# A hybrid decoder layer on one core: transposes two steps behind the scores, query tiles in the order 1, 3, 0, 4, 7, 6, 5, 2, w_out copied from step 6 and output pieces from step 15

## The reference, cut to what matters

```python
h = rmsnorm(x, norm_g) * (1.0 + scale) + shift        # shift, scale, gate from silu(c) @ ada_w + ada_b
z = h @ w_in                                          # x: 1024 rows (tokens) x 1024
xr, gr, q, k, v, ga, qi, ki, wi = split(z)
y_r = rg_lru(causal_conv(xr)) * silu(gr)              # 512 channels
# for each block of 128 queries, 8 heads of 64:
score = sum_h relu(qi_h . ki) * wi_h                  # indexer; causal
idx = top_k(score, 256)                               # keys that a query may see
p = softmax(q . k[idx] * 64 ** -0.5)                  # only those keys
y_a = (p @ v[idx]) * silu(ga)
y = concat([y_r, y_a]) @ w_out                        # 1024 x 1024
out = rmsnorm(x + gate * y, final_g)
```

## Time and profile before

| what | value |
|---|---|
| median of three runs | 598.59 us |
| the profiled execution | 599.06 us |
| its span, first to last instruction | 597.3 us |
| PE busy | 539.3 us, 90% |
| DVE, ACT, POOL busy | 419.9, 388.9, 211.3 us |
| first score of the attention stage | 340.59 us |
| first output piece | 400.67 us |
| last matmul ends | 590.0 us |

### The profile page before, as it was taken

The page is one execution under the profiler, slowest core; times in us unless marked ns, Lnnn a source line. Parts: engine busy times, 40 slices in busy tenths (PEclk is TensorE's granted clock), DMA queues, the critical chain, the costliest instruction groups (busy, mean ns, idle before and its releaser), DMA issues.

```text
span 597.3 us, 8271 instructions
## 1 busy us (share of the span) xinstructions
PE 539.3 (90%) x2756; PEld 447.6 (75%) x2758; DVE 419.9 (70%) x993; ACT 388.9 (65%) x690; POOL 211.3 (35%) x190
## 2 busy tenths in 40 slices
PE   0499988999999999989999866699999999999995
PEld 0477667888687777778888655678898989888874
DVE  4765659888989889998898757464566656664532
ACT  4572724554498898988898675673657566656631
POOL 6522044031436253588464000580412030314222
PEclk9869999999999999999999959679999999999998
DMA  8993094241011112134452160200102010101011
GB/s 304 397 326 102 19 253 165 57 106 36 12 61 36 36 36 52 48 99 120 106 130 82 29 254 1 82 26 1 41 31 72 1 59 13 42 31 71 1 72 70
DMA packets 19658, 51.98 MB, mean 87 GB/s; under 512 B 4128, under 2 KB 5152, under 8 KB 19616
## 3 DMA queue, kind: packets, MB, share of 16 engines
q1 hardware_dynamic: 19616, 51.45, 27.2%
HBM read 37.81 MB, written 4.19 MB: 70 GB/s over the span
## 4 chain that ended last, share of the span: by engine, by line
PE 73%; DVE 10%; ACT 6%; issue 5%; POOL 2%; DMA 2%; SPq 1%; DVEq 0%; POOLq 0%; ACTq 0%
PE pair L1542 28%; PE pair L1683 14%; PE pair L1705 6%; PE pair L1718 5%; PE pair L1511 4%; PE pair L1647 3%; PE pair L1648 2%; PE pair L1619 2%; DVE score_sb L1365 2%; PE pair L1727 2%; PE pair L1610 2%; PE pair L1611 1%; PE pair L1488 1%; PE pair L1743 1%; DVE tie L1299 1%
## 5 line engine op out<-in xcount | busy, mean ns | idle before, releaser
L1450 DVE TENSOR_TENSOR pt_lo<-pair,pt_hi 128x512 fp32r<-128x512 f32 (+3 forms) x96 | 50.5, 554 | 71.5 <-ACT pt_hi L1060 70.9
L955 ACT ACTIVATE bias_sb<-score_sb,tinies 128x1024 bf16<-128x1024 f32 (+2 forms) x93 | 95.7, 1032 | 4.2 <-DVE tinies L1234 3.9
L1542 PE MATMUL pair<-h_hi,w_hi 128*128 128x512 f32 x304 | 97.8, 403 | 0.0
L1542 PE MATMUL pair<-h_lo,w_hi 128*128 128x512 f32 x304 | 93.9, 390 | 0.0
L1542 PE MATMUL pair<-h_hi,w_lo 128*128 128x512 f32 x304 | 93.6, 389 | 0.0
L1220 DVE TENSOR_SCALAR_CACHE_REDUCE bias_sb<-score_sb,tinies 128x640 bf16<-128x640 f32 (+2 forms) x93 | 72.4, 801 | 0.8
L756 POOL TENSOR_SCALAR w_hi<-w_raw 128x1024 fp32r<-128x1024 f32 (+1 forms) x22 | 23.3, 1060 | 136.2 <-DMA w_raw<-in_w_tiles 115.3
L1542 PEld LDWEIGHTS pair<-h_hi,w_hi 128*128 128x128 f32 x304 | 56.3, 188 | 14.7 <-issue 4.6
L1542 PEld LDWEIGHTS pair<-h_lo,w_hi 128*128 128x128 f32 x304 | 57.1, 188 | 12.3
L1542 PEld LDWEIGHTS pair<-h_hi,w_lo 128*128 128x128 f32 x304 | 57.1, 188 | 12.2
L1060 ACT ACTIVATE pt_hi<-pair 128x512 fp32r<-128x512 f32 (+3 forms) x96 | 43.5, 489 | 28.2 <-PE pair L1718 25.9
(11 more groups left out here) (213 smaller groups left out, 1311.8 us busy)
## 6 DMA issues: line engine op xcount, KB each, us to landing
w_raw<-in_w_tiles SPq DMA_DIRECT2D x21, 512.0 KB, 4.0
ada<-in_ada_w SPq DMA_DIRECT2D x16, 512.0 KB, 12.1
x_sb<-in_x SPq DMA_DIRECT2D x8, 512.0 KB, 8.6
ada_g<-in_ada_w SPq DMA_DIRECT2D x8, 512.0 KB, 5.5
qs<-half_hi SPq DMA_DIRECT2D x16, 256.0 KB, 3.8
qs<-half_lo SPq DMA_DIRECT2D x16, 256.0 KB, 4.7
wo_raw<-in_w_out SPq DMA_DIRECT2D x8, 512.0 KB, 7.3
x_res<-in_x SPq DMA_DIRECT2D x8, 512.0 KB, 3.4
```

What stands on the lines that cost most here:

```text
L955: nc.scalar.activation(junk[i], score_sb[:, SCORE_OFF[i]:SCORE_OFF[i] + keys_of(i)], ACT.Sign, bias=cand[:, c:c + 1], scale=-1.0, accum_ou ...
L1450: nc.vector.tensor_tensor(pt_lo[:, 4 * b:4 * b + nc4, hh, :], psum[use % 2][:, 0:nc4 * P].rearrange("p (c q) -> p c q", q=P), f32(pt_hi[:, ...
L1542: ins = nc.tensor.matmul(psum[banks[half]][0:width, :], w[b][:, k, 0:width], hh[:, k, half * HALF:(half + 1) * HALF], start=(k == 0 and p ...
```

## The change

The lag of the transposes, and all lags that hang on it, grow by one step, so LAST_STEP goes from 77 to 78. The order of tiles becomes 1, 3, 0, 4, 7, 6, 5, 2: tile 3 (512 keys) takes steps 8 to 15, tile 0 (128 keys) 16 to 23, tile 4 (640 keys) 24 to 31. wo_hi copies run in steps 6 to 13. Output pieces begin at step 15 with pieces 0 and 1, and go on with one a step, piece g - 14, to step 77; yr_hi of the first two tiles moves to step 11. DVE waits at the first step of a tile for that tile's own mask alone, PE still for all six at the first step of tile 4, now step 24. prob_early grows to 512 keys, and the second tie_t buffer moves for it. fg_bc and yg lie over the queries of the tiles 1 and 3. ACT's Square writes its values, which nobody reads, into yg as float32 instead of a bfloat16 buffer, and DVE therefore waits before it writes yg again for that Square rather than for POOL's add.

```diff
@@ -98,11 +98,11 @@
-ATT = [1, 0, 4, 7, 6, 5, 3, 2]
-LAG_T = 1
+ATT = [1, 3, 0, 4, 7, 6, 5, 2]
+LAG_T = 2
 LAG_PV = LAG_T + 2
 LAG_O = LAG_T + 3
 LAG_Y = LAG_T + 10
@@ -115,8 +115,8 @@
 FLIP_AT = {3 + n: c for n, c in enumerate(MASK_ORDER)}
 RANK_AT = {4 + n: c for n, c in enumerate(MASK_ORDER)}
 BIAS_AT = {5 + n: c for n, c in enumerate(MASK_ORDER)}
-WO_START = 10
-OUT_START = 20
+WO_START = 6
+OUT_START = 15
 PIECES = {g: [2 * (g - OUT_START), 2 * (g - OUT_START) + 1] for g in range(OUT_START, 2 * OUT_START - LAG_OUT)}
 PIECES.update({g: [g - LAG_OUT] for g in range(2 * OUT_START - LAG_OUT, LAST_STEP)})
 PIECES.update({LAST_STEP - 8 + n: [56 + o] for n, o in enumerate((0, 1, 4, 5, 2, 3, 6, 7))})
@@ -375,7 +375,7 @@
         w_lo = [sb(f"w_lo{b}", R_W + 4096 * b, [P, KC, P], F32R) for b in range(3)]
         w_hi = [sb(f"w_hi{b}", R_W + 12288 + 4096 * b, [P, KC, P], F32R) for b in range(3)]
         prob = [sb(f"prob{b}", R_W + 4096 * b, [P, S]) for b in range(2)]
-        prob_early = sb("prob_early", R_W + 2048, [P, keys_of(1)])
+        prob_early = sb("prob_early", R_W + 2048, [P, keys_of(3)])
         pt_hi = sb("pt_hi", R_W + 8192, [P, NT, 2, P], F32R)
         pt_lo = sb("pt_lo", R_W + 16384, [P, NT, 2, P], F32R)
@@ -417,14 +417,12 @@
         gate_b = sb("gate_b", R_R + 4096, [P, D])
         v_raw = sb("v_raw", R_R + 8192, [P, NT, HD])
         tri = sb("tri", R_R, [P, S], BF16)
-        tie_t = [sb("tie_t0", R_R + 2048, [P, S], BF16), sb("tie_t1", R_W + 5120, [P, S], BF16)]
+        tie_t = [sb("tie_t0", R_R + 2048, [P, S], BF16), sb("tie_t1", R_W + 6144, [P, S], BF16)]
         x_res = [sb("x_res0", R_R, [P, D]), sb("x_res1", R_S, [P, D])]
         yr_hi = [sb(f"yr_hi{b}", R_S + 4096 + 2048 * b, [P, CT, P], F32R) for b in range(2)]
         pv_sb = [sb(f"pv{b}", R_R + 4096 + 1024 * b, [P, 2, P]) for b in range(2)]
         o_sb = sb("o_sb", R_R + 6144, [P, NH * HD])
         prob_late = sb("prob_late", R_S + 12288, [P, S])
-        sq_junk = sb("sq_junk", R_S + 16384, [P, HALF], BF16)[:, :]
         at = (R_R + 8192, R_S + 8192)
         ya_hi = [sb(f"ya_hi{b}", at[b], [P, 4, P], F32R) for b in range(2)]
         ya_raw = [sb(f"ya_raw{b}", at[b] + 2048, [P, 4, P]) for b in range(2)]
@@ -448,8 +446,8 @@
         gate_bc = sb("gate_bc", R_G, [P, D])
         gate_acc = sb("gate_acc", R_G, [P, D])
         q_free = sb("q_free", R_Q, [P, NH, S])
-        fg_bc = q_free[:, :, 0:P]
-        yg = [q_free[:, 4 * n:4 * n + 4, P:2 * P] for n in range(2)]
+        fg_bc = q_free[:, :, ATT[0] * P:ATT[0] * P + P]
+        yg = [q_free[:, 4 * n:4 * n + 4, ATT[1] * P:ATT[1] * P + P] for n in range(2)]
         ident = sb("ident", region(512), [P, P])
         fold = sb("fold", region(256), [P, HD])
@@ -1096,7 +1094,8 @@
                         act.wait_ge(rstd1_ok, ti)
                     if ti + half:
                         act.wait_ge(sq1_ok, 2 * ti + half)
-                    nc.scalar.activation(sq_junk, x_res[ti % 2][:, half * HALF:(half + 1) * HALF], ACT.Square,
+                    xs = x_res[ti % 2][:, half * HALF:(half + 1) * HALF].rearrange("p (c q) -> p c q", q=P)
+                    nc.scalar.activation(yg[half], xs, ACT.Square,
                                          accum_out=ssq[:, half:half + 1]).then_inc(sq1_ok, 1)
                     if half:
                         if ti + 2 < NT:
@@ -1391,8 +1390,8 @@
                 if g < 64:
                     i = ATT[g // 8]
                     n = keys_of(i)
-                    if g == 16:
-                        dve.wait_ge(bias_ok, len(PICK))
+                    if g % 8 == 0 and i in PICK:
+                        dve.wait_ge(bias_ok, MASK_ORDER.index(PICK.index(i)) + 1)
                     dve.wait_ge(att_ps, g + 1)
                     if g >= 3:
@@ -1417,7 +1416,7 @@
                     if ti + half == 0:
                         dve.wait_ge(gate_ok, 1)
                     if ti:
-                        dve.wait_ge(x1_ok, 2 * (ti - 1) + half + 1)
+                        dve.wait_ge(sq1_ok, 2 * (ti - 1) + half + 1)
                     nc.vector.tensor_tensor(yg[half], out_bank(ti, half).rearrange("p (c q) -> p c q", q=P),
                                             gate_bc[:, half * HALF:(half + 1) * HALF].rearrange("p (c q) -> p c q", q=P), ALU.mult).then_inc(y_ok, 1)
                     if ti == NT - 1:
@@ -1639,7 +1638,7 @@
                         pe.wait_ge(att_min, g - 1)
                     else:
                         pe.wait_ge(v_evac, 1)
-                    if g == 16:
+                    if g % 8 == 0 and i == 4:
                         pe.wait_ge(bias_ok, len(PICK))
                     for c in range(0, n, HALF):
                         w = min(HALF, n - c)
```

## The result

The changed kernel takes 601.38 us (median of 20 runs, 598.27 to 604.2) against 598.0 us of the kernel before, measured beside it (20 runs, 596.05 to 601.47): a ratio of 1.0048, 95% interval 1.0031 to 1.0064. The forecast was 3.3 us faster; it became about 3 us slower.

A forecast was written before the change was run, and what follows sets the result against it. Behind the clock dip PE alone bounds; time is the start of the pieces, plus PE work left, plus the tail. 8.7 - 3.4 - 2.0 = 3.3 us faster, from 598.59 to 595.3, range 590 to 600.5.

The forecast's parts named there:

- Term 1: Attention's mask steps: transposing the probabilities with a lag of two steps gains 1.25 us (bounds nothing and 2.3 us).
- Term 2: Steps 8 to 15: tile 3 in place of tile 0, 2.0 us later, last mask ending at 378.2.
- Term 3: From last mask to first output piece: 13.8 us instead of 23.3, the piece at 391.9, 8.7 us earlier.
- Term 4: PE work left when the first output piece starts: 3.4 us more, 26.8 against 23.4.
- Term 5: Behind PE's wait before piece 0: some 4 us of dense work at half clock, 2.0 us lost.
- At nothing: DVE's new wait, the f32 Square, tile 0's steps with pieces, the drain and moved buffers: taken as about no cost.
- (c): Tile 0's steps don't hide the pieces: 3.4 us a step instead of 2.1, 7.4 slower, 602.7; chance 0.10.
- (a): At piece 0: full clock, or an earlier piece; 5.3 us or more gained, 590 to 593.3; chance 0.20.
- (b): Steps 6 to 10: POOL's wo_lo blocks DVE's masks, up to 2.4 us a wait; 597 to 598.3; chance 0.20.

The follow-up runs named there:

- lag + start: The changed kernel with the old order of tiles put back (lag two, copies from step 6, pieces from step 15): ratio 1.0011 to the kernel before.
- lag, old order, pieces from 17: Lag two, old order of tiles, copies from step 6, pieces from step 17: ratio 0.9949 to the kernel before.

## Why the prediction was wrong

It said 3.3 us faster, and the stage became 2.9 us longer: 6.2 us apart. By its own terms:

- **Term 1** (lag in the masks, 1.25 us): right, 1.3 by the first tie transposes; 1.1 was left when step 5's min ended.
- **Term 2** (tile 3 in the mask steps, last mask 37.6 into the stage) is the step that failed first: 40.4. The lengths of scores and min were right, and that the masks' steps run at full clock was the silent assumption. The clock fell in step 8 instead of behind step 10, stretched the next two ranks and scores, and cost 2.7 us, which came back when PE was kept busy.
- **Term 3** (from the last mask to the first piece 13.8 us): 14.8. ACT began it a wo_hi late, since the exponential of step 10 had waited for PE at half clock, and POOL's last two wo_lo stood back to back, 4.70 us. The mechanism held, and PE waited 2.3 us for yr_lo rather than 4.
- **Term 4** (work left, 3.4): 4.3, by the account over what follows the first piece (192.7 us of work at full clock against 188.4). Ahead of the piece 3.1 less was done; the other 1.2 is what the whole stage has more, 219.2 against 218.0, as most rows with the new order have. Why they have it is open.
- **Term 5** (clock behind piece 0, 2.0): 1.7 by the account. The first two pieces took 4.27 us (397.37 to 401.64) instead of 2.79.
- **At nothing**: wrong. Behind the first piece PE waited 0.5 us for y and 2.2 for o_sb, against 0.8 before; all its idle time there is 2.7 us against 1.0, so 1.7 more. PE's steps are 2.5 us (19.9 for the eight from 402.60), with the rest of tile 3 in them. That the DVE's new wait is free and that the f32 Square costs nothing wasn't tried by itself; no wait of PE or DVE on it shows.

The first piece came 3.8 us later than forecast, and what follows it took 2.4 more than forecast: together the 6.2.

The number for rival (c) holds a slip: 10.7 us on the forecast of 595.3 are 606.0, 7.4 slower than before; 602.7 takes the 3.3 off twice.

Of the rivals, (a) fell with the clock. (b) did not happen in the changed kernel, by 0.2 us: the mask of step 7 began at 364.82 and took 0.26, the first wo_lo began at 365.02. I had placed the wo_lo 0.9 us ahead of the mask. With a lag of one, with either order of the tiles, the wo_lo did come first and held the mask by 1.8 to 1.95 us, in the very step that the forecast named. So the mechanism is real and its place was right, and the lag kept it off, which the forecast didn't count for the lag. (With lag, old order and early copies the mask of step 8 was held a little, 0.70 and 0.86 us instead of 0.43.) The ya_lo of 1.40 us at 388.86, beside a wo_lo, was held too; that it cost nothing is argued only from ACT being busy meanwhile. (c), the one slower case, was not the way: steps of tile 0 with pieces stayed at about PE's own time (PE is busy for 28.50 of the 30 us from 402.20 on). The way it did go slower was none of the four. The low clock in the mask steps is the step that weighs most. The deeper fault was in the sum: I counted how much earlier the first piece came and how much more work was left, two large numbers, and didn't ask what the difference means. It is the idle time and low clock taken away or added, and the forecast should have listed these gap by gap. It had 4 us of waiting ahead of piece 0 in it, written down and not priced.

What stays open: why the clock fell in step 8 in the changed kernel and with lag and order together, and one step later, or not before the last mask, in others, with gaps of nearly the same length. It is not the program alone: "lag + start" and "lag, old order, pieces from 17" issue the same instructions up to step 10, and in one the clock held until past the last mask (36.0 into the stage), while in the other it fell in step 9 and the mask ended at 38.2. Each is a single profile.

## What to carry to other kernels

Moving work earlier in an in-order queue gains only if its inputs are there: the pieces came 4.9 us sooner, PE stood for them, and starting them three steps later made the same kernel 0.43% faster. Moving work earlier on one engine can also set it beside another engine's work that excludes it: some 0.2 us decided whether a mask took 0.26 or 2.21 us. Where the bounding engine's work is constant, predict its idle time and clock loss, gap by gap, rather than the time of a milestone. Change one of several coupled constants at a time: the order cost 1.4% alone, which the early start and the lag partly hid, and the other two parts with a later first piece give 0.5%, with PE kept busy 0.85%.

## What the runs showed of the hardware

- Useless matmuls that keep PE busy between dependent steps raised the granted clock to 1.00 and shortened the changed kernel by 0.7%, and did nothing (1.0001) for the kernel before, where another chain set the steps.
- In the changed kernel the clock fell to 1.2 GHz in step 8, after an idle time of PE of 1.9 us and, before that, of 0.2 to 0.8 us at a time; in the early start alone and the order alone it held through such steps until past the last mask, and of two kernels with the same instructions up to step 10 it fell in one and not in the other.
- A one-input bf16 instruction of DVE from SBUF to SBUF waited for a POOL instruction to end: 1.79 us instead of 0.43, 2.21 and 2.07 instead of 0.26.
- A POOL sum of 128x1024 that reads one block twice took 1.89 us, where wo_lo with two different inputs takes 2.36.
